# A depthwise convolution of 31 taps: one channel block of four moved from VectorE to GpSimd, and the LayerNorm behind it put earlier

## The reference

```python
z = h @ w_in                                   # (tokens, 6656)
glu = ac * jax.nn.sigmoid(gc)                  # 512 channels
conv_out_c, new_hist_c = causal_dwconv(hist_c, glu, conv_c_w)      # 31 taps
yc = jax.nn.silu(layernorm(conv_out_c + conv_c_b, ln_c_g, ln_c_b))
merged = (gates[:, :, 0] * (ya @ w_branch[0]) + gates[:, :, 1] * (yb @ w_branch[1])
          + gates[:, :, 2] * (yc @ w_branch[2]))
x = x + gate1 * (merged @ w_out)
```

## Time and profile before

| | us |
|---|---|
| median of 3 runs | 4106.06 (4103.9 to 4109.76) |
| the profiled execution, its own time | 4103.9 |
| its span, first to last instruction | 4102.1 |
| busy in the span: PE, DVE, ACT, POOL | 4008.8, 2732.5, 1584.2, 812.4 |
| mean granted clock of PE | 0.995 of full speed |

### The profile page before, as it was taken

How to read it: one execution, slowest core, us unless ns; L and a number is a source line. 1 busy time by engine, 2 the same in 40 slices (tenths; PEclk the granted TensorE clock), 3 DMA queues, 4 the chain that set the end, 5 groups by cost and what they waited for, 6 DMA issues and landing times.

```text
span 4102.1 us, 77256 instructions
## 1 busy us (share of the span) xinstructions
PE 4008.8 (98%) x29632; PEld 3893.8 (95%) x29632; DVE 2732.5 (67%) x4453; ACT 1584.2 (39%) x2673; POOL 812.4 (20%) x685
## 2 busy tenths in 40 slices
PE   6999999999999999999999999999999999999998
PEld 3899999999999999999989999899999999999998
DVE  2367638977666636777753775698776664477776
ACT  2222323333577733333332223333337775333332
POOL 1000000000122206555300000000002221356551
PEclk9999999999999999999999999999999999999999
DMA  4444332354466668999934532225445667799995
GB/s 171 140 113 134 103 117 77 118 166 136 128 190 193 192 202 315 345 352 352 336 128 114 134 109 83 78 89 170 136 137 160 187 190 208 238 352 345 352 349 185
DMA packets 418219, 781.87 MB, mean 191 GB/s; under 512 B 151184, under 2 KB 274448, under 8 KB 417344
## 3 DMA queue, kind: packets, MB, share of 16 engines
q1 hardware_dynamic: 176640, 441.70, 33.4%
q10 hardware_dynamic: 194240, 196.10, 15.2%
q0 software_dynamic: 47104, 141.00, 9.5%
HBM read 655.79 MB, written 122.88 MB: 190 GB/s over the span
## 4 chain that ended last, share of the span: by engine, by line
PE 95%; DVE 3%; ACT 1%; DMA 1%; issue 1%; DVEq 0%; SPq 0%; ACTq 0%; POOLq 0%
PE pg L1515 20%; PE pg L1518 19%; PE pg L1516 19%; PE pm L1827 5%; PE pg L1829 4%; PE pg L1828 4%; PE pm L1829 4%; PE pm L1828 4%; PE pg L1827 4%; PE pm L1567 3%; PE pm L1779 2%; DVE ys L1179 1%; PE pm L1542 1%; PE pm L1743 1%; DMA merged<-stream 1%; PE pm L1551 1%
## 5 line engine op out<-in xcount | busy, mean ns | idle before, releaser
L1515 PE MATMUL pg<-a_hi,w_hi 128*128 128x260 f32 x6400 | 1684.6, 284 | 25.1 <-DVE a_lo L1025 14.4
L1516 PE MATMUL pg<-a_lo,w_hi 128*128 128x260 f32 x6400 | 1667.2, 282 | 0.0
L993 DVE TENSOR_TENSOR w_lo<-raw,w_hi 128x1024 fp32r<-128x1024 f32 x688 | 841.2, 1225 | 1003.8 <-ACT w_hi L886 703.0
L1518 PE MATMUL pg<-a_hi,w_lo 128*128 128x260 f32 x6400 | 1290.0, 283 | 0.5 <-issue 0.5
L1515 PEld LDWEIGHTS pg<-a_hi,w_hi 128*128 128x128 f32 x6400 | 1208.7, 189 | 41.1 <-issue 37.1
L1516 PEld LDWEIGHTS pg<-a_lo,w_hi 128*128 128x128 f32 x6400 | 1205.6, 188 | 0.3
L1518 PEld LDWEIGHTS pg<-a_hi,w_lo 128*128 128x128 f32 x6400 | 987.1, 189 | 0.3 <-issue 0.2
L886 ACT CAST w_hi<-raw 128x1024 fp32r<-128x1024 f32 x500 | 525.7, 1051 | 784.9 <-PE pg L1829 739.6
L570 POOL DMA_INDIRECT rows<-stream,at_v x256 | 282.1, 1102 | 766.0 <-DVE acc_tok L1442 317.7
L580 POOL TENSOR_TENSOR one_j<-one_j,g_lo 128x896 fp32r<-128x896 f32 x112 | 189.3, 1690 | 1034.9 <-ACTq L914 1034.9
L618 ACT ACTIVATE hid<-pg 128x260 f32<-128x260 f32 x512 | 170.7, 386 | 517.0 <-PE pg L1518 497.1
(11 more groups left out here) (234 smaller groups left out, 5598.3 us busy)
## 6 DMA issues: line engine op xcount, KB each, us to landing
raw<-stream SPq DMA_DIRECT2D x688, 512.0 KB, 4.1
hidden_dram<-hid SPq DMA_DIRECT2D x256, 196.0 KB, 3.5
gate_dram<-gate_buf ACTq DMA_DIRECT2D x28, 1792.0 KB, 11.0
hid_in<-hidden_dram ACTq DMA_DIRECT2D x64, 784.0 KB, 6.1
gate_in<-gate_dram ACTq DMA_DIRECT2D x64, 784.0 KB, 11.0
ada_raw<-stream ACTq DMA_DIRECT2D x76, 512.0 KB, 3.4
hid_tok<-hid SPq DMA_DIRECT2D x256, 64.0 KB, 3.6
rows<-stream,at_v POOLq DMA_INDIRECT x256, 7.3
```

What stands on the lines that cost most here:

```text
L993: tt(ring(False, s), raw[:, s], ring(True, s).bitcast(F32), ALU.subtract).then_inc(lo_ready, 1)
L1515: pe.matmul(outs[h], w[0], a[h][0], start=first, stop=False)
L1516: pe.matmul(outs[h], w[0], a[h][1], start=False, stop=False)
L1518: mm = pe.matmul(outs[h], w[1], a[h][0], start=False, stop=last)
```

## The change

Block c = 3 of the 31-tap convolution is computed by POOL, the moment `glu` is complete and its five DMAs are issued: one tensor_scalar with the bias, and then 30 times a tensor_scalar into a temporary row and a tensor_tensor that adds it, each waited for before the next is issued. A new semaphore, `conv_pool`, tells DVE. DVE keeps the 93 taps of blocks 0 to 2, now 3 in each of the four `T_BB` steps, and 5 or 6 in each step of pass 0 and in steps 0 to 3 of pass 1. All four sample convolutions go to pass 1 step 4, where DVE then waits for `conv_pool` and raises `conv_ready`. The LayerNorm's parts come earlier: PE's sum at step 6 instead of 9, the centring at 7 instead of 9, ACT's squares at 8 instead of 9, PE's sum of squares at 9 instead of 10. The root stays at step 10. The reciprocal goes from step 10 to 11, in front of the multiplication. Silu goes from pass 2 step 0 to pass 1 step 11.

```diff
-BB_TAPS = (4, 6, 6, 6)
-BR_TAPS = ((7, 7, 3, 6, 2, 2, 7, 7, 7, 6, 2, 2), (7, 7, 3, 6, 2, 2, 6, 6, 5, 0, 0, 0), (0,) * 12)
-SAMPLES_AT = ((0, 4), (0, 5), (0, 10), (0, 11))
...
-        past_mean = sb(taps, "past_mean", [P, SEQ])
+        pool_tmp = sb(taps, "pool_tmp", [P, SEQ])
...
+                c = BC - 1
+                w_c = p_("conv_c").rearrange("p (c w) -> p c w", c=BC)
+                own.link(pool.tensor_scalar(ys[:, 2, c, 0:SEQ], glu[:, c, 0:SEQ], w_c[:, c, 0:1],
+                                            p_("conv_c_b")[:, c:c + 1], ALU.mult, ALU.add))
+                for k in range(1, WC):
+                    own.link(pool.tensor_scalar(pool_tmp[:, :], glu[:, c, k:k + SEQ], w_c[:, c, k:k + 1], None, ALU.mult))
+                    own.link(pool.tensor_tensor(ys[:, 2, c, 0:SEQ], ys[:, 2, c, 0:SEQ], pool_tmp[:, :], ALU.add))
+                pool.sem_inc(conv_pool, 1)
                 own.restart()
...
# ACT
-                        if b == 1 and step == 9:
+                        if b == 1 and step == 8:
                             act.wait_ge(c_cent, l + 1)
...
-                        if b == 2 and step == 0:
+                        if b == 1 and step == 11:
                             act.wait_ge(c_norm, l + 1)
...
# DVE
-                taps = [(c, k) for c in range(BC) for k in range(WC)]
+                taps = [(c, k) for c in range(BC - 1) for k in range(WC)]
...
-                    conv_c(BB_TAPS[c])
+                    conv_c(3)
...
-                def root_of_c():
+                def normalise_c():
                     dve.wait_ge(c_std, l + 1)
                     own.link(dve.reciprocal(rstd[:, :], rstd[:, :]))
-
-                def normalise_c():
...
-                        conv_c(BR_TAPS[b][step])
-                        if (b, step) in SAMPLES_AT:
-                            conv_c_samples(SAMPLES_AT.index((b, step)))
-                        if b == 1 and step == 8:
+                        if b == 0 or b == 1 and step < 4:
+                            conv_c(5 + (step % 2))
+                        if b == 1 and step == 4:
+                            conv_c(99)
+                            for c in range(BC):
+                                conv_c_samples(c)
+                            dve.wait_ge(conv_pool, l + 1)
                             dve.sem_inc(conv_ready, 1)
-                        if b == 1 and step == 9:
+                        if b == 1 and step == 7:
                             centre_c()
-                        if b == 1 and step == 10:
-                            root_of_c()
                         if b == 1 and step == 11:
                             normalise_c()
...
# PE
-                        if b == 1 and step == 9:
+                        if b == 1 and step == 6:
                             pe.wait_ge(conv_ready, l + 1)
...
-                        if b == 1 and step == 10:
+                        if b == 1 and step == 9:
                             pe.wait_ge(mod_taken, (l + 1) * BATCHES + 1)
```

More of the change, by code:

```diff
@@ L127, in row_turns @@
     return l * -(-(PICKS - k % ROWS) // ROWS) + (k // ROWS + 1)
-BB_TAPS = (4, 6, 6, 6)
-BR_TAPS = ((7, 7, 3, 6, 2, 2, 7, 7, 7, 6, 2, 2), (7, 7, 3, 6, 2, 2, 6, 6, 5, 0, 0, 0), (0,) * 12)
-SAMPLES_AT = ((0, 4), (0, 5), (0, 10), (0, 11))
-assert sum(BB_TAPS) + sum(map(sum, BR_TAPS)) == BC * WC
 FIRST_ADD, LAST_ADD = 8, 124
@@ L362, in build @@
         early_out, late_out = sem("early_out"), sem("late_out")
-        conv_ready = sem("conv_ready")
+        conv_pool, conv_ready = sem("conv_pool"), sem("conv_ready")
         src_ready = sem("src_ready")
```

## The result

The changed kernel takes 4137.53 us, the median of 4 runs (4135.99 to 4138.16), against 4106.78 of the kernel before in the same runs: a ratio of 1.0076, 95% interval 1.006 to 1.0091. It is slower by 30.8 us, where +32 was forecast.

The account below looks back on a forecast made before the run. PE, 98% busy, was taken as the bound. Pass 0 waits 25.0, clock 3.0 and pass 1, LayerNorm and Silu 4.1 made +32.1 us on 4103.9, 4136.0; median 4138, range 4108 to 4168 (the forecast's own 4126 to 4160).

Parts of the forecast that it names:

- w: Time a DVE instruction with two SBUF inputs loses to one POOL instruction: POOL's mean 0.885 less 0.3, 0.58 us.
- wait at pass 0 step 5: PE waits 9.6 us a layer for the half of `pg` that DVE frees after step 4's branch products.
- wait at pass 0 step 6: PE waits 2.9 us a layer for the half that DVE frees first in step 5.
- clock in pass 0, a layer: Lower PE clock after the 9.6 us wait costs 1.5 us a layer, 0 to 2.1 at the ends.
- wait at pass 1 step 6: Moved samples stand in front of step 5's multiplication on DVE, so PE waits 3.4 us.
- wait at pass 2 step 2, for ACT: Silu at step 11 waits for the normalising; PE waits 1.4 us in layer 1, 5.1 (4.5 net) in layer 2.
- side by side: Rival: taps with a pointer scalar are not held by POOL; only the +4.1 us remain, 4110 us; chance 0.16.
- 27w - 6.1: PE's wait at pass 0 step 5: 27 DVE instructions each held w, less 6.1 us of slack; 9.6 us.
- 6w - 0.6: PE's wait at pass 0 step 6: 6w of holding on DVE, less 0.6 us of slack; 2.9 us.
- slow-POOL rival: POOL's instructions take 1.7 us or more each, w = 1.4, meeting pass 0 steps 6 to 11; 4193 us or more; chance 0.12.
- T + 16.6: When ACT frees the half of pass 2's first product, counted from T, the end of pass 1 step 11's products.
- T + 15.2: When PE wants that half for pass 2 step 2 in the first layer, T being the end of step 11's products.

Follow-up runs that it names:

- e10: Kernel before, nothing on POOL: ten taps moved to pass 0 steps 5 and 11, late reciprocal, two taps fewer at pass 1 step 3; 4098.35 us, ratio 0.9981.
- e1: Changed kernel without 60 of POOL's 61 instructions a layer, only the first with the bias left; 4116.49 us, ratio 1.0022.
- e2: Changed kernel with POOL's loop replaced by 150 memsets a layer, which write SBUF and read nothing; 4116.3 us, ratio 1.0023.
- e3: Changed kernel with POOL's 30 tensor_tensor replaced by tensor_scalar, so all 61 instructions have one tensor input; 4120.94 us, ratio 1.0034.
- e4: Changed kernel with POOL's 30 later-tap tensor_scalar replaced by tensor_tensor, so 60 instructions have two inputs; 4162.25 us, ratio 1.0133.
- e7: Kernel before with block 3 on POOL, DVE's 93 taps placed where a held DVE isn't late, reciprocal at step 11; 4102.45 us, ratio 0.9988.

## Why the prediction was right, and what in it was not

The sign and the mechanism came out. That the size came out so closely is in part luck, because two errors cancel. The prediction had PE wait 37.7 us more (25.0 in pass 0 and 12.7 behind it), 8.6 of old waits gone, and 3.0 for the clock. In the profiled execution PE waited 27.2 us (16.6 and 10.6). Without any wait the four stages would be 8.9 us shorter than before, as e10's are, and what is left of the +29.9 is 11.7 us beyond the waits, which the low clock's 12.1 us account for. So the waits were put 10.5 us too high and the clock 8.7 too low. By its own steps:

| step | predicted | measured |
|---|---|---|
| POOL's tensor_scalar, uncontended | 0.74 us | 1.57 |
| POOL's tensor_tensor, uncontended | 1.03 | 1.26 |
| loss of a DVE instruction, mean (w) | 0.58 (0.44 to 0.9) | 0.47 |
| wait at pass 0 step 5 | 9.6 | 6.5 |
| wait at pass 0 step 6 | 2.9 | none; 1.7 at step 11 |
| POOL's instructions done before pass 0 | 24 | 17 |
| end of POOL's chain | 350 | 374.4 |
| clock in pass 0, a layer | 1.5 (0 to 2.1) | 2.1 in layer 1, 1.9 + 1.7 in layer 2 |
| pass 0, both layers | +28.0 | +10.1 + 11.7 = +21.8 (e1) |
| wait at pass 1 step 6 | 3.4 | 3.4 |
| wait at pass 2 step 2, for ACT | 1.4 and 4.5 net | none, and 3.8 |
| clock behind the waits of passes 1 and 2 | nothing | 1.7 in layer 1, 3.0 + 1.7 in layer 2 |
| passes 1 to 2, both layers | +4.1 | +0.7 + 7.4 = +8.1 (e1) |
| sum | +32.1 | +29.9 |

**That POOL's reads hold DVE** is shown, by e1, e2 and the size of the effect in e3 and e4, and the rival "side by side" is thus refuted. Why the tensor_scalar, which works longer, takes less from a tap is open. That the loss is POOL's time less 0.3 us holds for the tensor_tensor alone.

**The size of w.** The prediction had every instruction of POOL held against one tap, a mean of 0.885 - 0.3. Instead the tensor_scalar is twice as long as its nearest row but costs its tap 0.31, and while the pair runs three taps pass, of which one goes free: (0.92 + 0.31) / 3 = 0.41 for taps. Over pass 0's path from DVE's split at 293.99 to the multiplication at 331.16 it is 37.2 us against 24.6 unhindered, thus 12.6 / 27 = 0.47 with the splits and `y_lo`:

```profile
293.99 1.23 DVE L996 TENSOR_TENSOR w_lo<-raw,w_hi 128x1024 fp32r<-128x1024 f32 x1 [3.81 <-ACT w_hi L615]
...
313.11 3.43 DVE L1257 TENSOR_TENSOR y_lo<-ys,y_hi 128x2080 fp32r<-128x2080 f32 x1
...
331.16 0.76 DVE L1243 TENSOR_TENSOR merged<-pg,sig 128x260 f32<-128x260 f32 x2
```

The arithmetic of the path was sound: its 27w - 6.1 gives 6.6 at 0.47, and PE waited 6.54. (w is read from this same path, so this confirms the slack of 6.1 and not w.) What it was fed was mis-sized. One of the 27 was also miscounted: the first tap of block 1 (L1179) has one input in SBUF, and took 0.79 us against 0.54.

**Step 6 and the chain's length.** 6w - 0.6 would be 2.2 us at w = 0.47, but PE itself lost about 2.1 in the window behind its first wait and came no sooner than its half was free. The chain of 30 pairs at 1.57 + 1.26 + 0.2 is 91 us even uncontended, not 66; only 17 of its instructions were done when pass 0 began, and it reached to 374. So it also met step 10 and 11, where PE waited 1.7. The slow-POOL rival had the durations nearly right (1.57 where it needed 1.7 for both forms) and yet not the time, because duration isn't what holds DVE.

**Passes 1 and 2.** The wait at step 6 of pass 1 was worked out to the tenth, with nothing for the clock behind it: that was the second mis-sized term, 1.7 us in the first layer and 3.0 in the second, with another 1.7 behind the wait for ACT. In the first layer Silu was not late for PE. ACT's timeline:

```profile
482.23 1.28 ACT L837 ACT_TABLE_LOAD   x1
491.04 2.96 ACT L837 ACTIVATE ys<-ys,par 128x520 f32<-128x520 f32 x4 [7.53 <-DVEq L1220]
494.25 1.28 ACT L621 ACT_TABLE_LOAD   x1 [0.25 <-ACT ys L837]
495.55 0.67 ACT L621 ACTIVATE sig<-pg 128x260 f32<-128x260 f32 x2
```

Silu's table load, which the prediction had put behind the wait for DVE, stands ahead of it, so that 1.28 of the T + 16.6 were not there: about T + 15.3 against PE's T + 15.2. In the second layer PE waited 3.8 where 5.1 - 1.28 gives exactly that.

**All that can be won.** The prediction said 4.3 us a layer of PE's waits, 8.6 in all. e10 won 8.9 over the four stages and 8.0 in the medians, with the same work on DVE as before. With the 31 taps on POOL, e7 won only 4.7 over the stages; no run made their leaving DVE worth more.

## What to carry to other kernels

Before work goes from VectorE to GpSimd, see whether both read SBUF at the same time, and price it by what each form of GpSimd's instruction takes from a waiting VectorE instruction, not by its duration. Then find the points where VectorE's lateness is paid: here 46 us of held taps cost 22 us of pass 0, and 33 us of them cost 2 (e7), where fewer taps stood ahead of the branch products. Behind each longer wait of TensorE, add what the low clock takes: here it was over a third of the whole loss. And where PE is at 98%, add up PE's waits before anything else: that sum is the whole gain, and putting the same instructions in another order may collect it.

## What the runs showed of the hardware

- GpSimd's tensor_scalar with a pointer scalar, 128x512 float32, took 1.57 us, longer than the tensor_tensor of the same size, 1.26; the chain's first instruction, a tensor_scalar that multiplies and adds, took 1.01, and a memset 0.53.
- In the meetings read above, the tensor_tensor cost a VectorE tap with two inputs in SBUF 0.92 us and the tensor_scalar 0.31. GpSimd's own instruction became 0.26 to 0.31 longer beside a tap; its tensor_scalar became 0.85 longer beside a split and 1.94 beside `y_lo`.
- A single wait of 3.4 us of PE was followed by a granted clock at the lower level for 3.4 us of work in one layer and for 6.0 in the other of the same program. So it cost 1.7 or 3.0 us more than its length. A wait of 1.8 at pass 0 step 11 was followed by 3.4 us at the lower level in the second layer, and one of 1.7 in the first layer by none.
- ScalarE's table load for Silu stood ahead of the wait for Silu's data, 1.28 us that lie beside the wait. This is not so everywhere: in the earlier trace rows the sigmoid's load at 474.37 comes after 5.85 us of waiting, with the sigmoid right behind it. What decides it was not tried.
